# A tenth place for the experts' weights, gate rows moved to the last part, and a sigmoid written in place

## The reference: what is computed

```python
def first_block(x, ...):
    mix = hybrid_mixer(h, w_in, ...)              # stick-breaking attention and HGRN2, sigmoid gates, w_out
    h = layer_norm(DEEPNORM_ALPHA * h + mix, ln1_g, ln1_b)
    ffn = moe(h, router_w, router_b, w_up, b_up, w_down, b_down)   # 32 experts, 4 for each token
    return layer_norm(DEEPNORM_ALPHA * h + ffn, ln2_g, ln2_b)

    # an expert
    hcat = xblk @ w_up[e] + b_up[e]               # 1024 x 2048
    x_glu = jnp.minimum(hcat[:, 0::2], 7.0)
    x_lin = jnp.clip(hcat[:, 1::2], -7.0, 7.0)
    act = x_glu * jax.nn.sigmoid(1.702 * x_glu) * (x_lin + 1.0)
    return act @ w_down[e] + b_down[e]            # 1024 x 1024

def second_block(x, c, ...):
    mod = silu(c) @ w_ada + b_ada
    sh1, sc1, g1, sh2, sc2, g2 = jnp.split(mod[:, None, :], 6, axis=-1)
    ...                                           # neighbourhood and latent attention, short convolution
    x = x + g1 * (mixed @ w_out)
    gt, up = jnp.split(ada_norm(x, norm2_g, sh2, sc2) @ w_gu, 2, axis=-1)
    return x + g2 * ((silu(gt) * up) @ w_down)
```

## Time and profile before

| | |
|---|---|
| median of 3 runs | 1529.42 us (1527.02 to 1530.88) |
| the profiled execution's own time | 1528.25 us |
| its span, first to last instruction | 1526.5 us |
| mean granted TensorE clock | 0.998 |
| TensorE busy | 1429.0 us (94%) |
| VectorE, ScalarE, GpSimd busy | 584.2, 449.3, 38.4 us |
| moved by DMA | 516.47 MB, mean 338 GB/s |

### The profile page before, as it was taken

How to read it: one execution, slowest core, us unless ns; L and a number is a source line. 1 busy time by engine, 2 the same in 40 slices (tenths; PEclk the granted TensorE clock), 3 DMA queues, 4 the chain that set the end, 5 groups by cost and what they waited for, 6 DMA issues and landing times. The chain is left out here.

```text
span 1526.5 us, 19835 instructions
## 1 busy us (share of the span) xinstructions
PE 1429.0 (94%) x8005; PEld 846.0 (55%) x8005; DVE 584.2 (38%) x978; ACT 449.3 (29%) x597; POOL 38.4 (3%) x80
## 2 busy tenths in 40 slices
PE   9999999999999999988988989889889999999998
PEld 9987898344334434323423433333333788888887
DVE  4985457211210211210210210210211685777765
ACT  5654543121111112111111111111111536553343
POOL 2000030000000000000000000000000022000000
PEclk9999999999999999999999999999999999999999
DMA  8597999899999999999999999999999461345552
GB/s 284 175 295 258 327 336 411 369 427 428 427 429 427 429 428 427 430 428 428 429 428 428 429 428 428 429 428 429 428 427 367 132 193 56 108 143 191 193 188 88
DMA packets 126918, 516.47 MB, mean 338 GB/s; under 512 B 6885, under 2 KB 95310, under 8 KB 102254
## 3 DMA queue, kind: packets, MB, share of 16 engines
q1 hardware_dynamic: 125998, 513.59, 84.6%
q10 hardware_dynamic: 864, 2.10, 0.4%
HBM read 514.62 MB, written 1.05 MB: 338 GB/s over the span
## 5 line engine op out<-in xcount | busy, mean ns | idle before, releaser
L1329 PE MATMUL ps<-ring,xg 128*64 128x512 f32 x1456 | 324.8, 595 | 25.7 <-DMA ring<-in_expert_w_up 22.7
L1478 DVE TENSOR_TENSOR glu<-ps,bupT 128x512 f32<-128x512 f32 x32 | 22.1, 692 | 720.0 <-PE ps L1338 720.0
L1329 PEld LDWEIGHTS ps<-ring,xg 128*64 128x64 f32 x1456 | 102.4, 137 | 242.5 <-issue 191.5
L88 ACT ACTIVATE hrow<-ps 128x1024 f32<-128x1024 f32 x32 | 32.8, 1024 | 473.4 <-PE ps L1329 473.4
L1354 PE MATMUL ps<-ring,act 128*64 128x512 f32 x608 | 136.3, 596 | 0.0
L2221 PE MATMUL ps<-h_halves,w_hi 128*128 128x512 f32 x352 | 124.2, 399 | 0.1
L2332 DVE TENSOR_TENSOR w_lo<-ring,w_hi 128x2048 fp32r<-128x2048 f32 x36 | 82.5, 2292 | 55.8 <-ACT w_hi L88 55.8
L1329 PE MATMUL ps<-more,xg 128*64 128x512 f32 x416 | 93.0, 595 | 8.7 <-DMA more<-in_expert_w_up 7.5
L2226 PE MATMUL ps<-h_halves,w_lo 128*128 128x256 f32 x348 | 97.7, 281 | 0.0
L88 ACT ACTIVATE w_hi<-ring 128x2048 fp32r<-128x2048 f32 (+1 forms) x38 | 70.8, 1865 | 70.8 <-PE ps L2226 34.6
L88 ACT ACTIVATE y<-ps 64x512 f32<-64x512 f32 x64 | 37.9, 592 | 182.0 <-PE ps L1354 181.6
(11 more groups left out here) (419 smaller groups left out, 2256.4 us busy)
## 6 DMA issues: line engine op xcount, KB each, us to landing
ring<-in_expert_w_up SPq DMA_DIRECT2D x91, 2048.0 KB, 36.8
ring<-in_expert_w_down SPq DMA_DIRECT2D x38, 2048.0 KB, 39.3
more<-in_expert_w_up SPq DMA_DIRECT2D x26, 2048.0 KB, 35.4
more<-in_expert_w_down SPq DMA_DIRECT2D x16, 2048.0 KB, 38.8
ring<-in_w_in SPq DMA_DIRECT2D x28, 1024.0 KB, 8.3
ring<-in_w_ada SPq DMA_DIRECT2D x24, 1024.0 KB, 5.8
x_xT_xn<-in_expert_w_up SPq DMA_DIRECT2D x11, 2048.0 KB, 36.8
ring<-in_w_gu SPq DMA_DIRECT2D x22, 1024.0 KB, 5.1
```

The costliest lines, as they stand in the source:

```text
L88: return nc.scalar.activation(out, x, ACT.Copy)
L1329: last = nc.tensor.matmul(up[a2 * CAP:(a2 + 1) * CAP, u, :], k.xg[:, q, h * CAP:(h + 1) * CAP], w[:, c:c + 512], start=(q == 0), stop=(q = ...
L1478: link(nc.vector.tensor_tensor(k.glu[:, :, :, :], g, b[:, 0].to_broadcast(wide), ALU.add))
```

## The change

Three edits, made together.

1. `PLACES` becomes 10. The tenth place (`SPLIT`, 9) is in two pieces of half a chunk: the first third of `k.wide`, where the gate rows and the diagonals lay, and `k.tenth`, a piece of SBUF that other tiles use until the output projection of `branches` is done. A chunk in it is loaded by two transfers of 1 MB, and its semaphore counts 32 and not 16. It is loaded first right behind places 7 and 8. `LOOPED` becomes 5 (60 chunks are a multiple of 10), so the loops of TensorE and SyncE have five pairs in the body and turn three times.
2. The gate rows are no longer made in `branches`. `gate_rows` multiplies a modulation column, read with stride 0 as a 128 x 128 stationary operand, with the identity, eight times for a row. `g2` is made in `second_mix` in place of two fills, and copied by ScalarE in two halves before `evacuate(2)`; `g1` at the head of `output`, where `g2` was. The fills read `k.bupT`, and two use other banks.
3. The sigmoid is written into `k.act[:, h]`, where the product then goes, and the tile `sigm` is gone.

```diff
-PLACES = 9
+PLACES = 10
-EXTRA, MORE = 5, 7
+EXTRA, MORE, SPLIT = 5, 7, 9
-LOOPED = 3
+LOOPED = 5
+TENTH_AT = 7568
...
-            for i in (MORE, MORE + 1):
+            for i in (MORE, MORE + 1, SPLIT):
                 load_expert(k, sp, a, 0, i)
...
-            def gate_row(half):
-                return nc.tensor.matmul(k.ps[:, half, :], k.ones[:, :], k.diag[0][:, half * 512:(half + 1) * 512],
-                                        start=True, stop=True)
...
-            pe.wait_ge(gd, 1)
             logits(0, range(4)).then_inc(log_done, 1)
-            gate_row(0)
             turn(1, 0)
             logits(1, (0,))
             turn(1, 1)
             logits(1, (1, 2, 3)).then_inc(log_done, 1)
-            gate_row(1).then_inc(gb_done, 1)
             pe.wait_ge(m_ready, 2)
...
-            for n, row in enumerate((GATE1, GATE2)):
-                for m in range(KD):
-                    ins = nc.scalar.activation(k.diag[n][:, m * P:(m + 1) * P], k.ident[:, :], ACT.Copy,
-                                               scale=k.mod[:, row + m:row + m + 1])
-            ins.then_inc(gd, 1)
...
-            act.wait_ge(gb_done, 1)
-            act_copy(nc, k.gB[:, 0, :], k.flat[:, 0:1024])
...
+def gate_rows(nc, k, row, banks):
+
+    for m in range(KD):
+        last = nc.tensor.matmul(k.ps[:, banks[m // 4], (m % 4) * P:(m % 4 + 1) * P],
+                                k.mod[:, row + m:row + m + 1].to_broadcast([P, P]), k.ident[:, :], start=True, stop=True)
+    return last
...
 def expert_chunk(k, i):
 
     i %= PLACES
+    if i == SPLIT:
+        return [k.wide[:, 0:TT * D], k.tenth]
+    v = expert_place(k, i)
+    return [v[:, 0:2048], v[:, 2048:4096]]
...
+def landings(place):
+
+    return 32 if place == SPLIT else 16
...
-    sp.dma_start(expert_chunk(k, i), src).then_inc(k.expert_in[i % PLACES], 16)
+    place = i % PLACES
+    if place == SPLIT:
+        for half, dst in enumerate(expert_chunk(k, place)):
+            sp.dma_start(dst, src[:, half * 2048:(half + 1) * 2048]).then_inc(k.expert_in[place], 16)
+    else:
+        sp.dma_start(expert_place(k, place), src).then_inc(k.expert_in[place], 16)
...
-                    nc.scalar.activation(k.sig[:, :, :, :], k.glu[:, :, :, :], ACT.Sigmoid, scale=1.702)\
+                    nc.scalar.activation(k.act[:, h], k.glu[:, :, :, :], ACT.Sigmoid, scale=1.702)\
                         .then_inc(sig_ready, 1)
...
-                        nc.vector.tensor_tensor(k.act[:, h], k.lin[:, :, :, :], k.sig[:, :, :, :], ALU.mult)\
+                        nc.vector.tensor_tensor(k.act[:, h], k.lin[:, :, :, :], k.act[:, h], ALU.mult)\
                             .then_inc(act_ready, 1)
...
-            fill(nc, k, 4, k.gB[:, 0, 0:512], 2)
+            gate_rows(nc, k, GATE2, (4, 7)).then_inc(k.gb_done, 1)
...
+            act.wait_ge(k.gb_done, 1)
+            for half in range(2):
+                act_copy(nc, k.gB[:, 1, half * 512:(half + 1) * 512], k.ps[:, 4 + 3 * half, :])
             evacuate(2)
...
-            for half in range(2):
-                last = nc.tensor.matmul(k.ps[:, 6 + half, :], k.ones[:, :], k.diag[1][:, half * 512:(half + 1) * 512],
-                                        start=True, stop=True)
-            last.then_inc(k.gb_done, 1)
-            fill(nc, k, 4, k.gB[:, 0, 0:512], 1)
+            gate_rows(nc, k, GATE1, (6, 7)).then_inc(k.gb_done, 1)
+            fill(nc, k, 4, k.bupT[:, 0:512], 1)
...
             act.wait_ge(k.gb_done, 2)
-            act_copy(nc, k.gB[:, 1, :], k.flat[:, 3072:4096]).then_inc(g2_copied, 1)
+            act_copy(nc, k.gB[:, 0, :], k.flat[:, 3072:4096]).then_inc(g1_copied, 1)
...
             low_w(L_OUT + 1)
+            dve.wait_ge(g1_copied, 1)
```

More of the change, by code:

```diff
@@ L913, in branches @@
     gate_ready, gT_done = sem("gate_ready"), sem("gate_turned")
-    gd, ang_ready = sem("gate_diag"), sem("angles")
-    gb_done = k.gb_done
+    ang_ready = sem("angles")
     gates, m, hT, xs = k.gates, k.xT, k.hT1, (k.xhi, k.xlo)
@@ L1192, in hidden_columns, with expert_place @@
     return slice((m // 4) * 1024 + 2 * (m % 4) + par, (m // 4 + 1) * 1024, 8)
+def gate_rows(nc, k, row, banks):
[3 more added lines that the diff above has]
+    return last
 def expert_chunk(k, i):
     i %= PLACES
+    if i == SPLIT:
+        return [k.wide[:, 0:TT * D], k.tenth]
+    v = expert_place(k, i)
+    return [v[:, 0:2048], v[:, 2048:4096]]
+def expert_place(k, i):
     if i == EXTRA:
@@ L1213, in expert_arrived @@
     place = i % PLACES
-    pe.wait_ge(k.expert_in[place], r * (16 * uses(place)) + turn * (16 * LOOPED * PAIR // PLACES) + 16 * (i // PLACES + 1))
+    per = landings(place)
+    pe.wait_ge(k.expert_in[place], r * (per * uses(place)) + turn * (per * LOOPED * PAIR // PLACES) + per * (i // PLACES + 1))
     return expert_chunk(k, i)
@@ L1324, in up_weights @@
                         chunk = expert_arrived(k, pe, r, turn, at * PAIR + h * UP_CHUNKS + q // 2)
-                    w = chunk[:, (q % 2) * 2048:(q % 2 + 1) * 2048]
+                    w = chunk[q % 2]
                     for u in range(2):
@@ L1348, in down_weights @@
                         chunk = expert_arrived(k, pe, r, turn, at * PAIR + 2 * UP_CHUNKS + 2 * h + j // 2)
-                    w = chunk[:, (j % 2) * 2048:(j % 2 + 1) * 2048]
+                    w = chunk[j % 2]
                     for kk in range(2):
@@ L1402, in _ @@
             scatter((1,))
-            fill(nc, k, 7, k.gB[:, 0, 0:512], 1)
+            fill(nc, k, 7, k.bupT[:, 0:512], 1)
         @blk.scalar
@@ L1612, in _ @@
                 last.then_inc(xnT_done, 1)
-                fill(nc, k, 7, k.gB[:, 0, 0:512], 1 + t)
+                if t == 0:
+                    pe.wait_ge(bm_out, 2)
+                fill(nc, k, 5 if t else 3, k.bupT[:, 0:512], 1 + t)
             pe.wait_ge(hT_ready, 4 + 2 * TT)
@@ L1713, in _ @@
             values(heads - 1)
-            fill(nc, k, 0, k.gB[:, 0, 0:256], 1)
+            fill(nc, k, 0, k.bupT[:, 0:256], 1)
         @blk.scalar
@@ L2112, in output @@
     x3_sq, x3_sum, mlp_done = sem("x3_squares"), sem("x3_sum"), sem("mlp_done")
-    g_sum, g2_copied = sem("gate_sum"), sem("gate2_copied")
+    g_sum, g1_copied = sem("gate_sum"), sem("gate1_copied")
     sig, a_ready, stored, y_ready = sem("gate_sigmoid"), sem("mlp_ready"), sem("stored"), sem("y_out")
@@ L2144, in turned @@
                     if t:
-                        fill(nc, k, 5, k.gB[:, 0, 0:512], fills)
+                        fill(nc, k, 5, k.bupT[:, 0:512], fills)
                     pe.wait_ge(ready, t + 1)
@@ L2179, in _ @@
                 if c == 2:
-                    pe.wait_ge(g2_copied, 1)
+                    pe.wait_ge(g1_copied, 1)
                 for i, q in enumerate(BLOCKS):
@@ L2489, in program @@
                           for n in ("in_hi", "in_lo"))
+        base = nc.sbuf_base
+        with nc.sbuf_tensor("under", [P, TENTH_AT], F32), nc.sbuf_tensor("tenth", [P, SLOT], F32) as v:
+            k.tenth = v[:, :]
         with ExitStack() as early:
@@ L2565, in program @@
                 first_mix(nc, k, a)
-                k.diag = [k.x[:, n, :] for n in range(2)]
                 branches(nc, k, a)
@@ L2589, in program @@
                 k.b_dn = k.y[0:E, :]
-                k.glu, k.lin, k.sig = (md(n, [P, 4, 2, CAP]) for n in ("glu", "lin", "sigm"))
+                k.glu, k.lin = (md(n, [P, 4, 2, CAP]) for n in ("glu", "lin"))
                 k.act = md("act", [P, 2, 4, 2, CAP])
+                assert nc.sbuf_base == -(-base // 32) * 32 + 4 * TENTH_AT
+                md("tenth_place", [P, SLOT])
                 experts(nc, k, a)
```

## The result

The changed kernel takes 1535.28 us (median of 5 runs, 1533.62 to 1536.00) against 1528.27 us of the kernel before on the same chip (5 runs, 1525.40 to 1530.88): ratio 1.0042, 95% interval 1.0028 to 1.0056. It is slower, by 7.0 us by the medians; the forecast was 1528.3 us, 1.1 us under the median of before on record then, and its range ended at 1533.0. The profiled execution took 1535.28 us, its span is 1533.5 us. Lines of the changed kernel have other numbers: `load_expert` is L1250 and L1252, the up products L1342, the down products L1367, the gather L893.

A forecast was written before the change was run, and what follows sets the result against it. The stream of the experts' weights was taken as the bound. 1528.25 - 4.9 + 2.2 + 1.5 + 0.1 = 1527.15 us for the profiled execution, 1.17 us under the median, so 1528.3 us; range 1524.2 to 1533.0.

The forecast's parts named there:

- The tenth place: Start of the experts' part: chunk 9 goes out right behind chunk 8, later chunks land one chunk earlier, -4.9 us.
- The 30.2 and 25 of the prediction: Experts' part: TensorE's waits for chunks, 30.2 us before the change, were to become some 25 us.
- The gate rows leave the first part: Before the experts: without its two long rows TensorE's clock falls near 256 us and returns early in the first gather, +2.2 us.
- Five pairs in the loop's body: Experts' loop: 2,500 instructions may be fetched each turn, 24 more fetches from a saturated stream, bounds 0 and 2.8, taken +1.5 us.
- brings nothing: Rival on the tenth place: no gain if halves move more slowly or TensorE's cushion sets the end; 1531.6 us, chance 0.06.
- a sign of error: In the profile after, a weight stream under 428 GB/s, from halves or fetches, would show the forecast wrong.
- The rest: Sigmoid, second block's products, copies and waits 0; the row at the head of the last part +0.1 us.
- the third, in its spread form: Rival: the larger body is fetched again, spread over engines, 0.12 us each to twice that; 1529.6 to 1532.8 us, chance 0.13.
- Its strong form, all through one engine: Rival: all code fetches go through one DMA engine, 0.94 us each, 22.6 us in place of 1.5; 1549 us, chance 0.07.
- the clock holds: Rival: the clock stays at full before the experts and the longer body's code costs nothing; 1524.5 us, chance 0.22.

The follow-up runs named there:

- experiment 1: The changed kernel with two fills of 512 columns on TensorE where the gate rows stood: 1533.59 us, ratio 1.0031 to the kernel before.
- experiment 4: The changed kernel with two fills, the tenth place used only for chunk 9, three pairs in the body and four turns: 1527.97 us, ratio 0.9996 to before.
- experiment 5: The changed kernel with two fills, the tenth place used for chunks 9 and 19 only, three pairs in the body: 1527.03 us, ratio 0.9989 to before.
- experiment 6: The changed kernel with nine places and three pairs in the body, leaving the moved gate rows and the sigmoid: 1531.58 us, ratio 1.0024 to before.
- experiment 2: The kernel before with all 15 looped pairs written out in the body, nothing else changed: 1534.20 us, ratio 1.0035.
- 12: The kernel before with a quarter of the up products cut into two of 256 columns, body 1,692, five turns: 1536.57 us, ratio 1.0046.
- experiment 9: The kernel before with half of the up products cut into two of 256 columns, body 1,884, five turns: 1538.32 us, ratio 1.0062.
- 10: The kernel before with all up products cut into two of 256 columns, body 2,268, five turns: 1540.17 us, ratio 1.0076.
- experiment 3: The kernel before with the chunks of one place loaded by two transfers of half a chunk: 1529.51 us, ratio 1.0003.
- experiment 8: The kernel before with 15 pairs in the body and the chunks of one place moved in two halves: 1535.13 us, ratio 1.0040.
- 7 (ten places): The changed kernel with two fills and 15 pairs in the body, ten places all through, no jump back: 1530.96 us, ratio 1.0018 to before.
- 11 (changed again): The changed kernel run once more with nothing altered: 1534.14 us, one run.

## Why the prediction was wrong

**The mechanisms were all named; the price of the code fetches and the cost of the halves, put at nothing, made most of the miss.** In the order of its steps:

*The tenth place, -4.9 us.* Right in its place. In experiment 1, where the clock does not interfere, chunk 10 lands 4.8 us earlier than before (279.08 against 283.87). The slack held: the waits for chunks are 30.6 us and were 34.2. (The 30.2 and 25 of the prediction leave out `k.wide`, 4.0 us of waits before; 29 was to be foreseen.) What the step does not say is that the gain needs the place for longer than the one chunk in the standstill: experiment 4 gives 2.65 us back at chunk 19, experiment 5, with a second use, nothing at chunk 29.

*The gate rows leave the first part, +2.2 us.* The mechanism was right and the size nearly: +3.1 us by the first refill, +3.0 us by the time of experiment 6 alone. The fall came at 256.7 us, near 256 as put. The return was put early in the first gather; it came at its end, 267.0 us, so the gather took 3.41 us in place of 2.15. The gather I had as +1.0 and it is +1.3; what stands ahead of it I had as +1.2 and it is +1.8, since VectorE's chain hid less of the logits and positions. The Trainium skill, TensorE: Matmul & The Clock Gate, part 1, has the lower level as the default that activity releases. The traces agree: the level fell while TensorE did 32-column passes and transposes, and it stayed where two products of 512 columns stood among them.

*Five pairs in the loop's body, +1.5 us.* **This is the step that failed.** The count was near: 24 more fetches expected, 28 measured (36 against 8). The price was not. I took 0.04 to 0.12 us each, from the stream's rate. The rate does say that: 286.12 MB in place of 287.01 MB in experiment 2, 0.09 us a fetch. But what counts is when a chunk is complete: its semaphore rises in 16 steps, as many as there are DMA engines, and TensorE waits for all of them. The table has the loss from chunk 45 to 180 by the last step (the landing) and by the first, nine and ten places alike:

| kernel | body | fetches 450 to 1120 us | loss by the last step, us | by the first, us | a fetch, us |
|---|---|---|---|---|---|
| before | 1,500 | 0 | 0.12 | 0.18 | |
| 6 (rows only) | 1,500 | 0 | 0.32 | 0.21 | |
| 4 (once) | 1,500 | 5 | 1.70 | 0.42 | 0.32 |
| 5 (twice) | 1,500 | 5 | 1.73 | 0.14 | 0.32 |
| 2 | 7,500, no jump back | 23 | 4.71 | 0.13 | 0.20 |
| 12 | 1,692 | 33 | 6.32 | -0.15 | 0.19 |
| 9 | 1,884 | 36 | 7.55 | -0.07 | 0.21 |
| 10 | 2,268 | 41 | 7.85 | -0.14 | 0.19 |
| 3 (halves) | 1,500 | 0 | 1.46 | 1.23 | |
| 8 (halves) | 7,500, no jump back | 23 | 5.94 | 1.14 | 0.19 |
| 7 (ten places) | 7,500, no jump back | 23 | 5.90 | 1.04 | 0.20 |
| 1 (ten places) | 2,500 | 27 | 6.73 | 0.92 | 0.20 |
| changed | 2,500 | 27 | 6.82 | 1.01 | 0.20 |
| 11 (changed again) | 2,500 | 27 | 7.28 | 1.08 | 0.22 |

In the last column the 0.12 us of before is taken off, and for the kernels with halves also 0.09 us for each split chunk (14 with ten places, 15 in experiment 8). The fetches leave the first step where it was, even 41 of them, and move the last: they delay some of a chunk's 16 shares and the chunk waits for the latest. The halves move both.

In experiment 2 the mean of the 16 steps loses 2.1 us more than in the kernel before, which is what the bytes say, and the last 4.6. By the bytes a fetch keeps its engine from the weights for 1.4 us (an estimate: 0.89 MB / 23 at a sixteenth of 428 GB/s; its packet alone takes 1.04 to 1.07 us on average in the traces, where the prediction had 0.94 from a rounded share). So five fetches that cost 1.6 us are one on the latest engine, and the 4.6 us of 23 are some three. So 0.2 us is no fixed price of a fetch but what it comes to when they are spread over the engines as here.

From some twenty fetches on it is 0.19 to 0.22 us each with jumps back and without, so the jumps cost the stream nothing that shows beyond their fetches. 28 fetches at 0.2 us are 5.6 us. By the times it is 5.3 us for 24 in experiment 2, 0.22 us each, and 0.19, 0.24 and 0.25 us in experiments 12, 9 and 10.

*The halves* stood in the prediction only as the rival "brings nothing" and as a sign of error, without a price. They take 0.09 us a split chunk by the landings, 1.6 us for the 18 behind chunk 10. By the times it is less sure: 20 split chunks cost 0.6 us in experiment 3 and 1.3 us in experiment 8 over experiment 2.

*The rest* held by the number: from the last landing to the end 353.96 and 354.00 us. The way there was not the forecast's, which kept the lower clock level at the head of `output` (1301.6 us before): in the changed kernel's trace that stretch is gone, and one of the same 3.4 us stands at 1198.8 us in `second_mix`. That the two come to the same is luck as far as the runs show.

**The sum again, from the runs:** -4.9 (place) + 3.1 (clock) + 5.6 (28 fetches) + 1.6 (halves) = +5.4 us, against 7.0 measured (5.7 in the one further run of the changed kernel, 1534.14 us against 1528.49). The 1.6 us that remain are of the size of what the last eleven chunks lose more: 3.18 us in the changed kernel and 3.13 us in experiment 1, against 1.50 us before. There too it is the last of the 16 steps that loses, the first only 0.15 us. But the other kernels have 1.5 to 3.5 us there, in no order of their fetches; what causes it was not found.

**The rivals.** The one that held in kind is the third, in its spread form: "at 0.12 each to twice that", 1529.6 to 1532.8 us. 0.20 us lies inside it, and its reason, that a chunk waits for its slowest part, is the one that the runs bear out; the halves and the clock's larger part took the time beyond. Its strong form, all through one engine, needs 0.94 us a fetch and is excluded by every row of the table. "The tenth chunk brings nothing" is excluded by experiment 1's landing, "the clock holds" by the trace.

## What to carry to other kernels

Where a stream of transfers sets the time, price everything that interrupts it by the landings and not by GB/s: a chunk is as late as its latest engine's share, here twice what the rate told (0.20 against 0.09 us a fetch). Before a loop's body is made longer, look at whether its code is still fetched after the first turn; a buffer that needs a longer body can cost more than it gives. Experiment 5 kept the short body and was 1.6 us faster than before, where the changed kernel was 7.0 us slower. And "TensorE would wait there anyway" does not make an instruction free: if it is the only long product in the stretch, taking it out can lower the clock for what stands behind it, here for 3 us.

## What the runs showed of the hardware

- A loop of 1,500 matmuls and weight loads (some 50 waits and register instructions more, 17 a pair) was not fetched again in 670 us; one of 1,692 was, with 33 fetches in the same time. The Trainium skill, Runtime: NRT & Kernel Launch, section Instruction fetch mechanics, gives TensorE room for 2,048 instructions. Taken as the size of a body that stays, as the prediction took it, the bodies of 1,692 and 1,884 would have stayed. They did not; the measurement decides.
- Behind a jump back to code that has to be fetched TensorE stood 2.0 to 2.7 us in 16 of 18 cases, 3.5 and 3.8 us in the other two (experiment 9). The same section says that such a branch waits for its fetch; the traces agree, 2.19 us at 543.8 us in the changed kernel and 2.46 us above. In the changed kernel no chunk near it landed more than 0.8 us late. In 5 of the 18 cases (experiments 9, 10 and 11) 3.4 us at the lower clock level began within the wait or up to 1.3 us behind it; experiment 2 has such stretches at 724.5 and 960.0 us without a jump, so the wait is not shown to be the cause.
- 64 more passes and as many weight loads a pair (experiment 9), with the same columns, left TensorE's busy time in the same 530 us nearly as it was, 477.8 us against 472.9 us.
